# Expert outputs scattered row by row from GpSimd instead of stored whole from ScalarE's queue

## What is computed

```
pg = softmax(x @ w_gr + b_gr);  g_idx = argmax(pg)           # one of 4 groups
pe = softmax(le[tok, g_idx]);   top_p, top_i = top_k(pe, 2)   # two of its 8 experts
gate = g_p * top_p / sum(top_p)
def expert_block(xe, e):
    return (silu(xe @ w_g[e]) * (xe @ w_u[e])) @ w_d[e]       # 1024 -> 256 -> 1024
y[token] = sum over its two experts of gate * expert(x[token])
h = LN(alpha * x + y)
```

## Time and profile before

| | |
|---|---|
| median of 3 runs | 3193.65 us (3191.0 to 3195.42) |
| the profiled execution, its own time | 3192.24 us |
| its span in the trace | 3190.0 us |
| PE busy | 2771.0 us, 87% of the span |
| DVE / ACT / POOL busy | 1426.2 / 790.1 / 653.8 us |
| chain that ended last | PE 75%, DVE 11%, ACT 3%, DMA 3%, issue 3% |
| line 820 (all products) in that chain | 68% |
| DMA moved | 503.08 MB, mean 158 GB/s |

### The profile page before, as it was taken

The page is one execution under the profiler, slowest core; times in us unless marked ns, Lnnn a source line. Parts: engine busy times, 40 slices in busy tenths (PEclk is TensorE's granted clock), DMA queues, the critical chain, the costliest instruction groups (busy, mean ns, idle before and its releaser), DMA issues.

```text
span 3190.0 us, 56735 instructions
## 1 busy us (share of the span) xinstructions
PE 2771.0 (87%) x22522; PEld 1551.8 (49%) x22522; DVE 1426.2 (45%) x3976; ACT 790.1 (25%) x1875; POOL 653.8 (20%) x651
## 2 busy tenths in 40 slices
PE   6998889989979959999399978999998899699980
PEld 3545566666655533333145456666666455233320
DVE  4112667666643462222451056666655335422227
ACT  0101354444431101111100024444444220011110
POOL 1000111111100025555310011111111000455534
PEclk9998899999989979999699969999999899799995
DMA  7113232322232439998731132333222225499956
GB/s 277 65 37 98 67 115 90 90 90 89 90 102 92 187 132 329 363 360 295 277 143 52 39 106 74 119 90 100 86 82 87 106 87 220 162 364 364 362 194 228
DMA packets 171844, 503.08 MB, mean 158 GB/s; under 512 B 48413, under 2 KB 89377, under 8 KB 146369
## 3 DMA queue, kind: packets, MB, share of 16 engines
q1 hardware_dynamic: 101760, 307.91, 28.3%
q0 software_dynamic: 50240, 120.23, 10.9%
q10 hardware_dynamic: 19584, 71.31, 5.7%
HBM read 629.93 MB, written 86.89 MB: 225 GB/s over the span
## 4 chain that ended last, share of the span: by engine, by line
PE 75%; DVE 11%; ACT 3%; DMA 3%; issue 3%; DVEq 3%; another core or an unknown queue 3%; POOL 0%; ACTq 0%; SPq 0%
PE ps L820 68%; PE ps L817 7%; DMA c_x<-xd 2%; DVE grams L2191 1%; DVE S_all L2655 1%; DVE uu L2191 1%; ACT PT L1663 1%; DVE c_x L2227 1%; DVEq L2656 1%; DMA c_b<-ybd,dga 1%; ACT kT L1663 0%; ACT S_all L1919 0%; DVE negm L2657 0%; DVE c_h L2205 0%
## 5 line engine op out<-in xcount | busy, mean ns | idle before, releaser
L820 PE MATMUL ps<-w_slots,xbT 128*64 128x512 f32 (+1 forms) x2048 | 462.2, 604 | 18.6 <-DVE xbT L3131 18.6
L820 PE MATMUL ps<-hT,w_in 128*128 128x512 f32 x896 | 390.6, 597 | 3.5 <-ACT hT L1663 3.5
L747 POOL DMA_INDIRECT xb<-xd,idall x256 | 256.9, 1004 | 153.0 <-issue 81.0
L820 PEld LDWEIGHTS ps<-w_slots,xbT 128*64 128x64 f32 x2048 | 144.9, 139 | 290.4 <-issue 271.4
L820 PE MATMUL ps<-w_out,o_mixT 128*128 128x512 f32 x576 | 261.9, 602 | 20.0 <-issue 18.7
L820 PEld LDWEIGHTS ps<-hT,w_in 128*128 128x128 f32 x896 | 171.0, 192 | 216.4 <-issue 211.0
L820 PE MATMUL ps<-w_slots,hidT 128*64 128x512 f32 (+1 forms) x1024 | 231.9, 593 | 3.8 <-issue 2.5
L820 PE MATMUL ps<-grams 64*64 64x64 f32 (+1 forms) x4624 | 187.1, 232 | 51.4 <-DVE grams L2191 21.9
L3131 DVE STREAM_TRANSPOSE xbT<-xb 128x1024 f32<-128x1024 f32 x64 | 79.7, 1245 | 337.7 <-DMA xb<-xd,idall 337.6
L820 PEld LDWEIGHTS ps<-grams 64*64 64x64 f32 (+1 forms) x4624 | 166.0, 145 | 81.6 <-issue 25.0
L820 PEld LDWEIGHTS ps<-w_out,o_mixT 128*128 128x128 f32 x576 | 107.4, 193 | 139.7 <-issue 137.9
(11 more groups left out here) (395 smaller groups left out, 4300.8 us busy)
## 6 DMA issues: line engine op xcount, KB each, us to landing
w_slots<-in_w_gu SPq DMA_DIRECT2D x64, 2048.0 KB
w_slots<-in_w_dn SPq DMA_DIRECT2D x64, 1024.0 KB
ybd<-yb ACTq DMA_DIRECT2D x64, 512.0 KB
pd<-stage SPq DMA_DIRECT2D x56, 256.0 KB, 2.6
out_y<-c_h ACTq DMA_DIRECT2D x27, 512.0 KB, 2.9
w_in<-in_w_in SPq DMA_DIRECT2D x6, 2048.0 KB, 25.6
o_mixT<-mixd SPq DMA_DIRECT2D x18, 512.0 KB, 4.5
o_h<-out_y SPq DMA_DIRECT2D x18, 512.0 KB, 4.9
```

What stands on the lines that cost most here:

```text
L747: pool.indirect_dma_start(xb[p % 2][:, 256 * q:256 * q + 256], None, x_quarters, bass.IndirectOffsetOnAxis(ap=idall[:, NE * q + p:NE * q + ...
L820: return pe.matmul(out, lhsT, rhs, start=start, stop=stop, skip_group_check=True)
```

## The change

Three things are changed.

1. ACT's `store` is gone. POOL gets `rows_out_of(l, p)`: it waits until DVE and ACT have filled `yb` with block p, and issues one indirect DMA that writes each used row of `yb` to its place in `ybd`; unused rows have a number beyond `CAP - 1` and are skipped. In POOL's loop it stands behind `dnA(p - 1)` and handles block p - 3; the last three follow the loop.
2. The row numbers `yrow` are made in the routing on DVE: one operation ahead of `r_who`, and four on 32 partitions each behind `rows`. `NOROW` becomes 4096, so that unused rows fall outside.
3. `ybd` is cleared once, in layer 0: 32 DMAs of 512 KB from the zero tile `stage[4]`, two or three behind each of the first 14 feature stores on SP's queue; SP's later wait on `zero_out` covers them. And `gather` takes only 32 rows for the ninth tile.

```diff
-NOROW = 2048
+NOROW = 4096
...
-        erow = sb("erow", [P, 1])
+        erow, yrow = sb("erow", [P, 1]), sb("yrow", [P, NE], I32)
...
+                if l == 0:
+                    sp.wait_ge(dve_m.sem, dve_m.at("init", "zero"))
                 for f in range(NF):
                     store_feature(l, 0, f)
+                    if l == 0:
+                        for n in range(NE * f // NF, NE * (f + 1) // NF):
+                            sp.dma_start(ybd[n * P:n * P + P].rearrange("p (h c) -> p h c", h=2), stage[4][:].unsqueeze(1).to_broadcast([P, 2, 512])).then_inc(zero_out, 16)
...
                 if l == 0:
-                    sp.wait_ge(zero_out, 48)
+                    sp.wait_ge(zero_out, 48 + 16 * NE)
                 load_tile(l, NPT)
...
+            def rows_out_of(l, p):
+                pool.wait_ge(dve_m.sem, dve_m.at(("moe", l), f"yb{p}"))
+                pool.wait_ge(act_m.sem, act_m.at(("moe", l), f"dn{p}"))
+                pool.indirect_dma_start(ybd[:], bass.IndirectOffsetOnAxis(ap=yrow[:, p:p + 1], axis=0), yb[:], None,
+                                        bounds_check=CAP - 1, oob_is_err=False).then_inc(yb_out, 16)
...
+                W = P if t < NPT else WS
                 for k, c in enumerate((c_a, c_b)):
-                    pool.indirect_dma_start(c[t % 3][:], None, ybd[:], bass.IndirectOffsetOnAxis(ap=dga[:, TILES * k + t:TILES * k + t + 1], axis=0)).then_inc(ya_in[t % 3], 16)
+                    pool.indirect_dma_start(c[t % 3][:W], None, ybd[:], bass.IndirectOffsetOnAxis(ap=dga[:W, TILES * k + t:TILES * k + t + 1], axis=0)).then_inc(ya_in[t % 3], 16)
...
                     rows_in(l, p)
                     guA(l, p)
                     dnA(l, p - 1)
+                    if p == 3:
+                        pool.wait_ge(dve_m.sem, dve_m.at(("route", l), "out"))
+                    if p >= 3:
+                        rows_out_of(l, p - 3)
                 dnA(l, NE - 1)
+                for p in range(NE - 3, NE):
+                    rows_out_of(l, p)
                 pool.wait_ge(yb_out, 16 * NE * (l + 1))
...
-                def store(p):
-                    act.wait_ge(dve_m.sem, dve_m.at(k, f"yb{p}"))
-                    act.wait_ge(act_m.sem, act_m.at(k, f"dn{p}"))
-                    act.dma_start(ybd[p * P:p * P + P], yb[:]).then_inc(yb_out, 16)
...
-                    if p:
-                        store(p - 1)
...
-                store(NE - 1)
...
+                dve.tensor_scalar(yrow[:], rcst[:, Q_FIRST:Q_FIRST + NE], cst[:, C_ROW:C_ROW + 1], None, ALU.add)
                 tt(r_who[:], till.unsqueeze(1).to_broadcast([P, NE, NE]), bc(nth, [P, NE, NE]), ALU.is_lt)
...
                 tt(rowA[:], who, has, ALU.add).then_inc(dve_m.sem, dve_m.mark(k_, "rows"))
+                for q in four:
+                    r = slice(32 * q, 32 * q + 32)
+                    m = dve.scalar_tensor_tensor(yrow[r], idall[r, NE * q:NE * q + NE], -4.0 * TOK, yrow[r], ALU.add, ALU.max)
+                m.then_inc(dve_m.sem, dve_m.mark(k_, "out"))
```

More of the change, by code:

```diff
@@ L290, in plan @@
         T["act"].plan(("route", l), ["e1", "e2"])
-        T["dve"].plan(("route", l), ["E7", "E8", "oh0", "oh1", "part", "ids", "rows"])
+        T["dve"].plan(("route", l), ["E7", "E8", "oh0", "oh1", "part", "ids", "rows", "out"])
         T["pe"].plan(("moe", l), ["gu0"])
@@ L609, in _ @@
                 if l == 0:
-                    sp.wait_ge(dve_m.sem, dve_m.at("init", "zero"))
                     for q in range(2):
```

## The result

The changed kernel takes 3417.3 us (median of 4 runs, 3410.9 to 3421.7), the kernel before 3194.5 us beside it (4 runs, 3191.0 to 3197.5): ratio 1.070, 95% interval 1.068 to 1.072. It is 7% slower. The profiled execution has a span of 3414.3 us, 224.3 us more than before.

The account below looks back on a forecast made before the run. PE was taken to bound the expert stage, narrowly ahead of DMA. 3192.2 + 125 (loop) - 5 (gaps) + 1 = 3313 us profiled, 3315 us as median; own range 3275 to 3425, whole range 3187 to 3425 us.

Parts of the forecast that it names:

- the loop: Expert stage: copy of block q releases scatter, then gathers, transpose and next copy; one turn 7.1 us + L.
- the likeliest turn: Expert stage: copy to next copy takes 13.4 us, 2.6 us over PE's block; 24 turns, twice, +125 us.
- the copy and its semaphore: 0.65 + 0.1 us: Expert stage: time from the start of DVE's copy into `yb` until POOL's scatter is released.
- 7.81 less the store's part = 6.3 us: Expert stage: L taken from a gather behind a full weight burst, less the removed store's 0.52 MB at 356 GB/s.
- L: Expert stage: time from the last gather's issue to the start of its transpose, put at 6.3 us.
- Wrong: a granted clock under 1.00 in the stage.: Expert stage: PE's clock, 1.00 before; a lower one was named as a sign against the prediction.
- The first rival: Expert stage: the loop stays hidden under PE's 10.82 us, L under 3.7 us; 3188 to 3194 us, chance 0.22.
- The second rival: Expert stage: the scatter's landing holds the next copy into single `yb`; decides above 12.7 us, 3315 us and above, chance 0.05.
- Clearing 0: First projection: clearing `ybd`, 47 us of DMA, is hidden beside PE's work and costs 0.
- the third rival: First projection: clearing not hidden, evictions wait for a `stage` buffer; up to +47 us, chance 0.05 without the loop.
- The tail: End of the expert stage: an indirect DMA and its landing replace the store; -0.5 to +5 us a layer, taken as 0.
- The 5 us that fewer bytes should give back by PE's gaps: Expert stage: less DMA work per block removes PE's gaps, 2.5 us a layer, -5 us.

Follow-up runs that it names:

- wait alone: Kernel before, with GpSimd waiting for both engines' copies of block p - 3 into `yb`, nothing scattered or cleared: 3263.1 us, ratio 1.024.
- empty scatter: Changed kernel with ScalarE's whole store back and all row numbers of the scatter out of bounds, so it moves nothing: 3417.7 us, ratio 1.068.
- thin weights: Changed kernel loading only an eighth of each expert's weights from the sixth block of a layer on: 3181.6 us, ratio 0.998.

## Why the prediction was right, and where its sum was not

**The sign, the mechanism and its place: right.** The forecast was 3315 us, its own range 3275 to 3425, and the time is 3417. The rows named as the sign of it are there: PE waits ahead of down products, GpSimd waits for DVE's copy ahead of the scatter, the first projection ends where it did (`rowt<-pm` at 285.08 us, 285.74 before). The wait alone makes the loop, moving the scatter behind the gathers takes the loss back, and thinning the weights hides it. But the time lies at the upper end of the range, since the likeliest turn, 13.4 us, was 15.1 and 15.4: 214 us instead of 125. That it lies inside the range at all is partly luck, as the second step below shows.

**The step "the copy and its semaphore: 0.65 + 0.1 us" was mis-sized.** Copy to scatter is 1.46 us (1365.73 to 1367.19). GpSimd needs about 0.7 us between its release and an indirect DMA (0.77 us from the end of the copy with the wait alone). I had taken the semaphore's 0.1 us from engines that compute. It is 0.7 us of each turn, 34 us in all.

**The step "7.81 less the store's part = 6.3 us" for L was the wrong one.** With PE at full clock the burst goes out at 4.65 us and the last gather at 6.75 us, the geometry the prediction drew (4.3 and 6.0), and there L is 8.6 us: higher than the row of the full burst, not lower. That half a MB of store more or less does nothing is shown by the empty scatter (L 7.3 us with the store back) and by the table of four kernels (7.5 us with a store, 7.4 without, at the same place of the burst). Had every turn been like this, it would be 16.5 us, above the upper bound of 15.7, and 48 such turns would give some 3465 us, outside the range (an estimate: 48 x 5.7 us on the kernel before). The mean L of 7.2 to 7.5 us comes from something that I had excluded.

**"Wrong: a granted clock under 1.00 in the stage."** It is 0.93, and the prediction had named this as a sign against itself. It is none: the loop makes PE stand still for 5 us, the clock falls for the down product behind it, and this delays the burst. By the table of the burst's place it goes with shorter turns, not longer ones. This is read from one trace: no run kept the clock at 1.00 and the burst where it was. The DMA share of "about 0.8" is 0.67, which follows from the longer turn.

**How the 214 us split.** The wait alone has 84 us of them in the two stages. Of the 130 left, copy to first gather is longer by 1.23 us a turn, the scatter's slot, 48 x 1.23 = 59 us; L is longer by 1.1 and 1.5 us, 62 us; 9 us are left over. The growth of L goes with the burst's place (with the wait alone it goes out 0.6 to 0.9 us behind the last gather on average, in the changed kernel 0.8 us ahead): the slot pushes the gathers behind the burst. The scatter's packets ahead of the gathers are no rival to this. Without a burst they add at most 0.3 us (thin weights), and with one in flight, at the same place of the burst, L is 7.4 us with a scatter and 7.5 us without.

**The first rival is out.** It needed L under 3.7 us while weights stream; of 40 turns one came under that, with the burst behind the last gather. The Trainium skill's "DMA: Bandwidth & Descriptors", section on queues, rings and completion order, has the engines take turns between the queues; by that rule, as the prediction read it, gathers issued 2 us behind a burst would not wait for it. The trace disagrees: L is 8.6 us there, and 2.8 to 3.05 us when the weights are thin.

**The second rival was nearer than its 0.05 said.** It did not decide here: the scatter of 1350.86 had landed by 1354.19, where ScalarE's copy could start ([6.01 <-DMA ybd<-yb,yrow] in its timeline), and DVE's was due at 1365.73. With the first loop gone, the scatter's landing, 7.0 us on average, is what the copies wait for, and with 10.7 us from copy to landing on average it fits under PE's 10.8 us by next to nothing.

**The small terms.** Clearing 0: right (1.000 with the clearing alone), and with it the third rival is out. The routing's 0.2 us: nothing to see. The tail: 0 taken from ends of -0.5 and +5; it is +4.9, the upper end, less 2 us that the gathers behind it give back. I had compared the landing of the scatter alone, and not asked what ScalarE would issue earlier once its store was gone; whether those loads are the cause stays open. The 5 us that fewer bytes should give back by PE's gaps can't be seen in the changed kernel. With the scatter behind the gathers the down products' idle time is 1.4 us in all, against 3.8 us before: the gaps were smaller than the 5 us that I had put them at, and 2.4 us is what closing them gave. A time this small can't be told apart between kernels here.

## What to carry to other kernels

Before a wait is put on a queue, list what stands behind it in that queue, and follow each item until it returns to whoever ends the wait. If it returns, there is a loop, and its turn has to be priced with every issue on it and with the slowest landing that its own timing produces. Place a waiting DMA behind those that others are waiting for: here moving one DMA behind four others was 7% of the time. And skipping rows of an indirect DMA saved bytes only here, so it can pay only where bytes are the bound.

## What the runs showed of the hardware

- An indirect DMA whose 128 rows are all skipped cost what one with 66 used rows of 4 KB did: 1.0 us of GpSimd, the same number of packets, and 7.5 us from issue to the gather that waits for it at the end of a stage (1649.29 to 1656.77), against 7.2 us (3328.47 to 3335.69).
- GpSimd took some 0.7 us from the release of a wait to the start of an indirect DMA (0.77 us from the end of the copy waited for); a computation started after 0.09 us, and with its 0.55 us ahead of the DMA that was 0.84 us.
- Four gathers of a quarter of the columns came out 2.8 us after the last one's issue in quiet, 8.6 us when 3 MB of weights were issued 2 us ahead of it, some 7.4 us when they were 0.7 us ahead, and 3.3 to 4.4 us when they were 0.5 to 1.1 us behind; the scatter in front of the gathers made no difference to this that could be seen.
- After 5.2 us without work, PE's next 16 products took 6.70 us with 0.54 of the clock granted; after 2.5 us they took 3.76 us at 1.00. In the changed kernel every down product after more than 4 us of idleness was slow (5.0 to 6.7 us) and none after 3.4 us or less (3.9 us at most). With the wait alone one was slow after 2.65 us (5.46 us), so the length of the pause is not all of it.
